# Stick-breaking attention: transposes a slot later, VectorE's row work ahead of the q and k subtractions

## The reference, cut to what matters

```
z = einsum('bhqd,bhkd->bhqk', q, k) * scale
log_stay = where(before, log_sigmoid(-z), 0)
log_pass = cumsum(log_stay, reverse) - log_stay
a = where(before, exp(log_sigmoid(z) + log_pass), 0)
out = einsum('bhqk,bhkd->bhqd', a, v)
```

## Time and profile before

| | |
|---|---|
| median of 3 runs | 1502.61 us (1502.57 to 1506.66) |
| profiled execution: its own time | 1504.89 us |
| profiled execution: span of its instructions | 1503.1 us |
| TensorE busy | 1399.4 us, 93% of the span |
| VectorE, ScalarE, GpSimd busy | 715.2, 532.3, 384.3 us |
| mean granted TensorE clock | 0.971 of full speed |

### The profile page before, as it was taken

How to read it: one execution, slowest core, us unless ns; L and a number is a source line. 1 busy time by engine, 2 the same in 40 slices (tenths; PEclk the granted TensorE clock), 3 DMA queues, 4 the chain that set the end, 5 groups by cost and what they waited for, 6 DMA issues and landing times.

```text
span 1503.1 us, 18354 instructions
## 1 busy us (share of the span) xinstructions
PE 1399.4 (93%) x6848; PEld 1160.8 (77%) x6848; DVE 715.2 (48%) x850; ACT 532.3 (35%) x948; POOL 384.3 (26%) x244
## 2 busy tenths in 40 slices
PE   5889898989899998699799999999999999999995
PEld 4778787878778787588578888888888888888884
DVE  6477786868686878723221303132221313222138
ACT  5546565656565566332222121212111121211113
POOL 4110101101010103336225131323223142322325
PEclk9999999999999999799799999999999999999998
DMA  4000000000000001312002010211111020111102
GB/s 182 29 28 15 29 15 29 15 28 28 15 28 14 28 15 43 126 43 70 15 29 69 30 56 28 70 42 56 42 42 56 28 70 29 69 42 42 56 14 113
DMA packets 18336, 66.66 MB, mean 44 GB/s; under 512 B 2032, under 2 KB 2032, under 8 KB 18288
## 3 DMA queue, kind: packets, MB, share of 16 engines
q1 hardware_dynamic: 16560, 59.78, 11.5%
q10 hardware_dynamic: 1728, 6.29, 1.3%
HBM read 61.87 MB, written 4.19 MB: 44 GB/s over the span
## 4 chain that ended last, share of the span: by engine, by line
PE 86%; DVE 7%; ACT 3%; issue 2%; DMA 1%; POOL 0%; DVEq 0%; ACTq 0%; POOLq 0%
PE bank L1134 11%; PE bank L1133 11%; PE bank L1135 11%; PE bank L980 5%; PE bank L982 5%; PE bank L981 5%; PE bank L1181 5%; PE bank L1180 5%; PE bank L1182 5%; PE bank L1084 4%; PE bank L1056 2%; PE bank L1059 2%; PE bank L1058 2%; PE bank L1104 2%; PE bank L1103 2%
## 5 line engine op out<-in xcount | busy, mean ns | idle before, releaser
L681 POOL TENSOR_TENSOR w_lo<-raw,w_hi 128x1024 fp32r<-128x1024 f32 x89 | 219.2, 2467 | 819.4 <-ACT w_hi L421 819.1
L1133 PE MATMUL bank<-hnT_hi,w_hi 128*128 128x512 f32 x704 | 277.2, 394 | 2.9 <-DVE hnT_lo L782 2.9
L1134 PE MATMUL bank<-hnT_lo,w_hi 128*128 128x512 f32 x704 | 278.4, 395 | 0.0
L1135 PE MATMUL bank<-hnT_hi,w_lo 128*128 128x512 f32 x704 | 275.9, 392 | 0.0
L913 DVE TENSOR_TENSOR sg<-bank,sg 128x512 f32<-128x512 f32 x44 | 30.5, 692 | 437.7 <-ACT sg L614 437.7
L421 ACT ACTIVATE w_hi<-raw 128x1024 fp32r<-128x1024 f32 x89 | 93.4, 1061 | 404.5 <-PE bank L1135 353.5
L858 DVE TENSOR_TENSOR_SCAN stay<-stay,diag_one 128x256 f32<-128x256 f32 (+7 forms) x128 | 203.4, 1589 | 5.8 <-ACT stay L541 5.2
L429 ACT ACTIVATE AT_hi<-bank 128x512 fp32r<-128x512 f32 (+1 forms) x160 | 89.1, 557 | 223.3 <-PE bank L1084 222.4
L927 DVE TENSOR_TENSOR y<-bank,y 128x512 f32<-128x512 f32 x176 | 119.3, 690 | 94.4 <-PE bank L1182 93.1
L1133 PEld LDWEIGHTS bank<-hnT_hi,w_hi 128*128 128x128 f32 x704 | 132.8, 189 | 34.7 <-DVE hnT_lo L782 3.5
L980 PE MATMUL bank<-hnT_hi,w_hi 128*128 128x512 f32 x384 | 157.2, 409 | 1.5 <-DVE hnT_lo L782 1.5
(11 more groups left out here) (100 smaller groups left out, 2174.0 us busy)
## 6 DMA issues: line engine op xcount, KB each, us to landing
raw<-in_units SPq DMA_DIRECT2D x98, 512.0 KB, 3.3
acc<-in_x SPq DMA_DIRECT2D x8, 512.0 KB, 8.6
x_in<-in_x ACTq DMA_DIRECT2D x8, 512.0 KB, 3.4
out<-y SPq DMA_DIRECT2D x7, 512.0 KB, 2.6
g_pre_s<-in_mix_pre ACTq DMA_DIRECT2D x1, 512.0 KB, 5.5
g_post_t<-in_mix_post ACTq DMA_DIRECT2D x1, 512.0 KB, 5.9
g_ffn_t<-in_ffn_pre ACTq DMA_DIRECT2D x1, 512.0 KB, 3.4
g_out<-in_ffn_post ACTq DMA_DIRECT2D x1, 512.0 KB, 3.4
```

What stands on the lines that cost most here:

```text
L681: nc.gpsimd.tensor_tensor(w_lo[slot], raw[:, raw_slot, :], w_hi[slot].bitcast(F32), ALU.subtract).then_inc(w_ready, 1)
L1133: nc.tensor.matmul(bank_ap, wh, hnT_hi[:, kt, cols], start=(kt == 0), stop=False)
L1134: nc.tensor.matmul(bank_ap, wh, hnT_lo[:, kt, cols], start=False, stop=False)
L1135: mm = nc.tensor.matmul(bank_ap, wl, hnT_hi[:, kt, cols], start=False, stop=(kt == KT - 1))
```

## The change

`T_LAG` goes from 6 to 7. All that hangs on a transposed chunk moves with it: AV, the slots of `vT` and of v's transposes, and the output copies; the tail gets a tenth slot, while the output projection keeps its slots 1 to 8. Double buffers are now picked by `(s - T_LAG) % 2` or `(n - T_LAG) % 2`, since the lag is odd. On VectorE, `row_work` now stands ahead of `projections` within a slot.

```diff
-T_LAG = 6
+T_LAG = 7
-V_SLOT = {5: 0, 8: 1}
+V_SLOT = {6: 0, 9: 1}
-VT_SLOT = {4: 0, 7: 1}
+VT_SLOT = {5: 0, 8: 1}
-O_SLOT = {18: 0, 8: 1}
-TAIL_SLOTS = 9
-WO_TAIL = {s: [(n // 16, n % 16 // 8, n % 8) for n in range(4 * (s - 1), 4 * s)] for s in range(1, TAIL_SLOTS)}
+O_SLOT = {19: 0, 9: 1}
+TAIL_SLOTS = 10
+WO_TAIL = {s: [(n // 16, n % 16 // 8, n % 8) for n in range(4 * (s - 1), 4 * s)] for s in range(1, 9)}
...
@@ vector engine, step @@
-                            t_lo_sub(g, AT_lo[:, s % 2, 0:w], TB[n % 2][:, 0:w], AT_hi[:, s % 2, 0:w])
-                    if not tail:
-                        projections(p, par, s, first, proj)
+                            t_lo_sub(g, AT_lo[:, (s - T_LAG) % 2, 0:w], TB[(n - T_LAG) % 2][:, 0:w], AT_hi[:, (s - T_LAG) % 2, 0:w])
                     for n, kind, k in row_work(s, first, tail):
...
                             nc.vector.tensor_tensor(a, a, st, ALU.mult).then_inc(row_done, 1)
+                    if not tail:
+                        projections(p, par, s, first, proj)
```

More of the change, by code:

```diff
@@ L521, in step @@
                             t_hi_copy(g, V[:, 4 * at:4 * at + 4, 0, 0:3:2, :],
-                                      TB[n % 2][:, :].rearrange("p (k h c) -> p k h c", k=4, h=2))
+                                      TB[(n - T_LAG) % 2][:, :].rearrange("p (k h c) -> p k h c", k=4, h=2))
                         elif kind == "a" and not (first and s < T_LAG) and not (tail and s >= T_LAG):
@@ L527, in step @@
                             _, w = t_blocks(GROUPS[at // GROUP][1], at % GROUP)
-                            t_hi_copy(g, AT_hi[:, s % 2, 0:w], TB[n % 2][:, 0:w])
+                            t_hi_copy(g, AT_hi[:, (s - T_LAG) % 2, 0:w], TB[(n - T_LAG) % 2][:, 0:w])
                     if not tail:
@@ L549, in step @@
                         qk_hi(step_units(p, "q")[0], "q", 1 - par, 0, ACCB[0])
-                    if s == 18:
+                    if O_SLOT.get(s) == 0 and not tail:
                         o_copy(p, 0)
-                    if s == 8 and not first:
+                    if O_SLOT.get(s) == 1 and not first:
                         o_copy(p - 1, 1)
@@ L842, in step @@
                             t_lo_sub(g, V[:, 4 * at:4 * at + 4, 1, 0:3:2, :],
-                                     TB[n % 2][:, :].rearrange("p (k h c) -> p k h c", k=4, h=2),
+                                     TB[(n - T_LAG) % 2][:, :].rearrange("p (k h c) -> p k h c", k=4, h=2),
                                      V[:, 4 * at:4 * at + 4, 0, 0:3:2, :])
@@ L1054, in step @@
                             vl = V[:, j, 1, h:h + 2, :].rearrange("p a c -> p (a c)")
-                            hi, lo = AT_hi[:, s % 2, c0:c0 + w], AT_lo[:, s % 2, c0:c0 + w]
+                            hi, lo = AT_hi[:, (s - T_LAG) % 2, c0:c0 + w], AT_lo[:, (s - T_LAG) % 2, c0:c0 + w]
                             nc.tensor.matmul(dst, vl, hi, start=(z % (SLOTS // 2) == 0 and m == 0), stop=False,
@@ L1070, in step @@
                             for q in range(4):
-                                mm = nc.tensor.transpose(TB[n % 2][:, q * P:(q + 1) * P],
+                                mm = nc.tensor.transpose(TB[(n - T_LAG) % 2][:, q * P:(q + 1) * P],
                                                          vT[:, q * P:(q + 1) * P], ident[:, :])
@@ L1083, in step @@
                                     src = ROW_OFF[x][k] + P * (j - ROWS[x][k])
-                                    mm = nc.tensor.transpose(TB[n % 2][:, c0 + q * P:c0 + (q + 1) * P],
+                                    mm = nc.tensor.transpose(TB[(n - T_LAG) % 2][:, c0 + q * P:c0 + (q + 1) * P],
                                                              A[:, h, src:src + P], ident[:, :])
```

## The result

The changed kernel takes 1456.44 us (median of 4 runs, 1454.86 to 1458.33) against 1504.63 us (median of 4, 1502.57 to 1507.51) for the kernel before: a ratio of 0.9679, 95% interval 0.9655 to 0.9703, or 48.2 us less. The forecast was 1458 in 1450 to 1472, counted from a median of 1502.61 us for the kernel before.

The account below looks back on a forecast made before the run. TensorE, busy 93% of the span, was taken as the bound, so removing its waits and low clock pays. 39.6 + 9.4 + 0.3 - 4.5 = 44.8 us off 1502.61 gives 1457.8, predicted 1458 us, range 1450 to 1472.

Parts of the forecast that it names:

- The waits of the middle steps: Slots 11 and 16: the transposes' waits, hand-overs and lost clock all go, 6.6 us a step, 39.6 us over six.
- Each of the two edits attacks it: Transposes' wait for VectorE's product: the longer lag and VectorE's new order each work against it.
- the lag alone just covers the wait: Slot 11: with lag seven transposes are asked for at about 164, the product having ended at 163.58.
- In the middle steps AV never waits now: Before the change AV had no waits for AT_lo in middle steps; none was expected to replace the transposes' waits.
- I take 0: New AV waits after the change: 0 us, bounded by 0 and 2 us in each of seven steps, 14 us.
- the place that I watched: Slot 18: AT_lo ended 0.26 us before AV wanted it; the new order was to make the margin some 2 us.
- Step 0: First attention step: three waits of 5.54 us, their hand-overs and 2 x 1.7 us of clock go, 9.4 us.
- Step 7: From slot 7 on VectorE is the bound and its work is unchanged, so only 0.3 us is gained.
- the 5 us allowed: Step 7: bounds either way on its time, because VectorE's collisions with GpSimd's operations are dealt anew.
- the 3 us: Sign of error: step 7, from slot 7 to the output projection's first part (48.5 us), changing by over 3 us.
- The tail's end: Ahead of tile 2: four parts of cover instead of eight lose 2.8 us, plus 1.7 us of clock, 4.5 us.
- The sum: Whole kernel: 39.6 + 9.4 + 0.3 - 4.5 = 44.8 us gained.

Follow-up runs that it names:

- the order alone: Kernel before with only VectorE's projections put behind the row work, lag kept at six: 1455.2 us, ratio 0.9677.
- the lag alone: Changed kernel with the k and q subtractions back in front of the scans and products, lag of seven kept: 1468.53 us, ratio 0.9757.
- the q subtractions ahead: Kernel before (lag six) with only the k subtractions moved behind the row work, the q subtractions staying ahead of it: 1458.95 us, ratio 0.9691.
- the second trace: Changed kernel run again unaltered, on the chip of its parts: median 1456.37 us, ratio 0.9677; its profiled execution 1458.22 us.
- the memset: Changed kernel with GpSimd's eight subtractions of step 7 replaced by memsets that read nothing, leaving out the lo halves of W_o: 1442.83 us, ratio 0.959.
- the parts a slot later: Changed kernel with the output projection's 32 parts in tail slots 2 to 9 instead of 1 to 8: 1451.34 us, ratio 0.9643.

## Why the prediction was right, point by point

*The waits of the middle steps.* Right in place and mechanism. The term was 6.6 us a step; 6.90 came. By slots, from first score to first score: slot 10 shrank by 2.92 us (2.70 + 0.16 forecast), slot 11 by 1.66 (1.7 of clock), slot 15 by 2.08 (1.88 + 0.16). That is 6.66, and the order alone gave 6.62; the remaining 0.24 to 0.28 is the share of the lag whose cause I did not find. My 65.4 was a further 0.15 too high because I read the step as 72.0, the width of my window, where the scores repeat every 71.85.

*"Each of the two edits attacks it", "the lag alone just covers the wait".* True of the product, wrong as a statement on time: the lag alone moves the lateness from the transposes to AV (1.47 us a step). Each edit alone does end the transposes' waits of the middle steps: the lag alone gives 36.1 us, the order alone 49.5. With the new order the lag is nearly superfluous. The order takes away the cause that the earlier trace rows show, VectorE idle in front of work that it could have done; the lag only gives the late product more time.

*"In the middle steps AV never waits now", "I take 0".* Right for the changed kernel, but the place that I watched was not the critical one. I had named slot 18, with 0.26 us of margin (and slot 20 for the lag alone); the lag alone waited in slot 17 and the q subtractions ahead gave no wait at slot 20. With the new order neither matters. VectorE's work did not stay at 54.65 us a step either: it is 51.92 in 65 us, as fewer of its scans and products meet a `w_lo`.

*Step 0.* 9.4 us forecast, 11.66 measured in the first pair of traces, 9.0 in the second one (68.55 - 59.52). By slots, the waits and the clock behind them gave 9.3 of the 11.66 (slots 5, 10, 11, 15 and 16: 0.83, 3.30, 1.34, 2.20 and 1.65), so the term was right. The rest is 1.36 of clock in slot 0, which is luck, and the chunk that left step 0, 1.0 us, which I had counted as 0 net, with its loss in the tail.

*Step 7.* 0.3 us forecast, 1.44 measured (1.99 in the second trace), inside the 5 us allowed. It is not the 0.3 us that I named: the order alone leaves step 7 at 72.23 us, so this gain comes with the lag, which deals the collisions anew. From the first score of slot 7 to the first part it is 50.07 us before (578.01 to 628.08) and 49.12 after (523.70 to 572.82), within the 3 us. VectorE is busy for 46.00 of 46.00 us, so it is the bound as I said (before, its chain was not quite without a gap: it idled for 0.63 and 0.17 us). That GpSimd's operations stretch it was an argument there; the memset shows it, with 13 us.

*The tail's end.* 4.5 us forecast, 3.61 + 1.65 = 5.3 measured, of which 3.16 are the longer wait (3.58 against 0.42 us; I forecast 2.8 more) and 1.34 the clock behind it (the first eight parts of tile 2 take 7.04 us against 5.70; I forecast 1.7), together the 4.5. The other 0.8 are the chunk that came into the tail, 1.0 us, less 0.6 by a better clock behind the first part in this execution (0.91 against 0.72 in its second three us), and 0.3 us further on whose place is not shown. With the parts a slot later tile 2's wait is 0.68 us and its first eight parts take 5.70; of the 5.0 us that this recovered a good part lies at the tail's front.

*The sum.* 44.8 us forecast, 48.2 between the medians, 50.0 between the two profiled executions. No term of the sum failed. That the time itself, 1458 against 1456.44, came nearer than the gain is luck: it was counted from 1502.61 us, and the kernel before has 1504.63 in the four runs; from there it would have been 1459.8. Against the 50.0 the 5.2 us are 1.8 from the middle steps, 2.3 from step 0, 1.1 from step 7 and 0.8 from the start, less 0.8 in the tail.

## What to carry to other kernels

When the longest wait of the bound engine names a second engine that was itself idle just before the late instruction, look at what its in-order stream waits for there: an instruction that doesn't depend on that wait should stand ahead of it, and here this was worth more (49.5 us) than a longer lag between the stages (36.1 us), which hid the lateness in one place and moved it to the next consumer. Look for each such gap at the clock behind it as well: here 1.7 us were lost behind 2.70, nothing behind 1.88. And after any shift of a pipeline by a slot, look at its end: the cover of the last serial chain is shifted too, and here it cost a tenth of the gain until the parts were moved along.

## What the runs showed of the hardware

Matmuls without any use made the kernel before 11.3 us faster, since with its gap cut from 2.70 to 0.39 us the granted clock stayed at 1.00 in place of 0.57. Behind a wait of 3.58 us the next 24 matmuls of 512 columns took 7.04 us, behind 0.68 and 0.42 us they took 5.70 (clock 1.00).

The granted clock over the first ten us of the attention was 0.73, 0.83 and 1.00 in three executions with the same instructions of TensorE ahead of them, worth 2.6 us between the first and the last: that much of a difference between two single executions says nothing.

A scan of VectorE that meets a subtraction of GpSimd takes 3.20 us in place of 1.22; one of 1.48 us into which a memset of 0.95 us falls keeps its length, and so do the k subtractions (0.69 us), which take an input from PSUM, beside a subtraction. In step 7, with eight such subtractions, this costs 13 of 71 us, more than the two edits' whole effect on step 0 and far more than what was left to gain in the tail.
